# Modulation rows of a hybrid Hyena / FNet / RG-LRU layer on four column groups of the TensorE array

## The chip, the cores and the metric

The kernel runs on one NeuronCore of one Trainium2 chip. The metric is the device time of one launch in microseconds (us), lower is better; each number of a kernel is the median of several runs. For this kernel three runs gave 2820.89 us (2819.37 to 2822.51).

## The reference, cut to what matters

One layer is applied to 1024 latent and 256 context tokens with 1024 channels: a norm with modulation, an input projection that feeds three mixers (a Hyena long convolution, FNet, a bidirectional RG-LRU), their merge, and a SwiGLU block. What the change touches is the modulation alone, six vectors of 1024 values for each of two conditions (latent, context):

```python
mod_ctx = jax.nn.silu(c_ctx[None, :]) @ w_ada[l] + b_ada[l]     # w_ada: 1024 x 6144
mod_lat = jax.nn.silu(c) @ w_ada[l] + b_ada[l]
...
sh1, sc1, g1, sh2, sc2, g2 = jnp.split(mod[:, None, :].astype(dt), 6, axis=-1)
h = rmsnorm(x, n1) * (1 + sc1) + sh1
```

So a product of 2 x 1024 by 1024 x 6144 in fp32, with the result needed channel by channel on the partitions.

## The kernel before, in words

Channels lie on the 128 partitions, tokens along the free dimension. There is one hand-written program for each engine, tied by semaphores; a `wait_ge` holds its whole engine.

The modulation goes through the program in 24 half groups of 256 columns. `csilu` holds silu of both conditions, 8 blocks of 128 channels by 2. `ada_row_unit` (L891) multiplies, for each half group, the 8 blocks `csilu[:, k, :]` (stationary, 128 x 2) with `ada_w[:, k*256:...]` (moving, 128 x 256), all accumulated in rows 0 and 1 of a PSUM bank. ScalarE copies these two rows to `ada_row` in SBUF (L1196, L1259). `ada_turn_unit` (L901) turns them: 128 columns of `ada_row` are the stationary operand, a 2 x 2 identity the moving one, and the result is 128 partitions x 2. VectorE adds the bias into `mod` (`ada_add`, L1504).

Eight half groups are made in the setup, while x is loaded and its squares are summed. The other sixteen are made two at a time in the eight passes of the first stage, `l1_pass` (here "L1 stage", 116 to 575 us). In each pass TensorE's own order is:

- the row unit for two half groups (16 products), then one product `ones` x `ss_k` (L974),
- a wait for `fa_ready`, which VectorE gives at the end of a butterfly (`first_stage`: some forty small VectorE operations at L244 to L256, signalled at L1650), then 24 small DFT products (`fwd_unit`, L953),
- products that make filter taps (`taps_units`, L965), and the input projection of one tile (`projection_tile(2i+1)`, L860 to L862),
- a second wait for `fa_ready`, 24 more DFT products, the turn unit (L906), and the projection of the next tile (`projection_tile(2i+2)`).

ScalarE's order in a pass: copy the rows (L1259), take the root `rs_k` (L1263), copy three pieces of a finished projection from PSUM into `hin` (L1247), which lets GpSimd start; later the copy of a second projection, then the squares of the taps.

GpSimd (POOL) splits each weight tile into a high and a low part (L789, L792) when the projection before it is done, and then computes the short convolution of every other tile (`hy_conv`, L798): it waits for ScalarE's copies into `hin` (L802), and runs two scalings (L805) and ten pairs of a scaling (L811) and an addition (L813).

VectorE's order in a pass: sums and squares of taps (L1643, L1646), butterfly (L244 to L256) and `fa_ready`, a difference (L1651), a reciprocal (L1653), scaled DFT results into `kstage` (L1616), butterfly again and `fa_ready`, taps (L1629), two memsets (L1637, L1638), `kstage` again, the bias addition of the modulation (L1504), the convolution of the other tile (L1588, L1593).

Of the kernel before, what the change touches and what calls it, by code (L numbers as in the profile page):

```python
# [11 lines left out]
ACT = mybir.ActivationFunctionType  # L31
AX_X = mybir.AxisListType.X

P = 128
D = 1024
KD = D // P
# [13 lines left out]
FILT_EMB, FILT_HID = 17, 64  # L50
# [3 lines left out]
HALF_GROUPS = 24  # L54
ADA_FIRST = 8
SQUARES_AT = ((0,), (1, 2), (3, 4), (5,), (6,), (7,), (), ())
FIRST_MIX = 3
MIX_BANKS = 5


V_N1, V_N2, V_FG, V_BADA = 0, KD, 2 * KD, 3 * KD
V_HY = V_BADA + 48
V_LAM = V_HY + 64
V_ALL = V_LAM + 2 * KD

R_CONV, R_CONVB, R_BR, R_BI, R_ST = 512, 516, 517, 519, 521
R_ALL = 523


# [9 lines left out]


TWO_PI = [6.28125, 0.0019350051879882812, 3.0199e-07]
# [6 lines left out]

def real_dft_even(o, z, temp, out):


    e, d = temp(0, 4), temp(4, 8)
    o.add(e, z(0, 4), z(4, 8))
    o.sub(d, z(0, 4), z(4, 8))
    o.sub(out("re4"), temp(0), temp(2))
    o.sub(out("im4"), temp(3), temp(1))
    o.add(temp(8, 10), temp(0, 2), temp(2, 4))
    o.sub(temp(10), temp(5), temp(7))  # L100
    o.add(temp(11), temp(5), temp(7))
    o.add(out("re0"), temp(8), temp(9))
    o.sub(out("re8"), temp(8), temp(9))
    o.mul_add(out("re2"), temp(10), COS[2], temp(4))
    o.mul_add(out("re6"), temp(10), -COS[2], temp(4))
    o.mul_add(out("im6"), temp(11), -COS[2], temp(6))
    o.mul_sub(out("im2"), temp(11), -COS[2], temp(6))


# [26 lines left out]


def real_dft_context(o, z, out):
# [4 lines left out]
    o.mul(out("cim1"), z(1), -1.0)  # L143


# [44 lines left out]


def inverse_context(o, b, temp, y):
# [5 lines left out]


class Chain:  # L200

# [8 lines left out]
    def loose(self, ins):  # L212


        ins.then_inc(self.sem, 1)
        self.n += 1
        if self.n > 1:
            self.eng.wait_ge(self.sem, self.n - 1)
# [15 lines left out]


class Butterfly:

# [17 lines left out]


class MixUnits:

# [15 lines left out]


def places(buf, width, first=0):  # L280
# [8 lines left out]


def spectrum_places(buf):


    def at(name):
        if name.startswith("c"):
            return buf[:, 9 + int(name[3:]), :] if name[1:3] == "re" else buf[:, 19, :]
        f = int(name[2:])
        return buf[:, f if name[:2] == "re" else 11 + f, :]
    return at


# [12 lines left out]

HAS_IMAG = [1 <= q <= 7 or q == 10 for q in range(FH)]
IMAG_AT = {q: (19 if q == 10 else 11 + q) for q in range(FH) if HAS_IMAG[q]}
PAIRS = [(1, 2), (3, 4), (5, 6), (7, 10)]
SINGLES = (0, 8, 9, 11)  # L320


def build_program(nc, dr):

    ctx = ExitStack()
    with ctx:
# [3 lines left out]
        def sb(stack, name, shape, dt=F32):  # L330
            return stack.enter_context(nc.sbuf_tensor(name, shape, dt))


# [5 lines left out]
        vec = sb(ctx, "vec", [P, V_ALL])  # L339
# [10 lines left out]
        cvec = sb(ctx, "cvec", [P, KD, 2])  # L350
        csilu = sb(ctx, "csilu", [P, KD, 2])
        ps = [ctx.enter_context(nc.psum_tensor(f"ps{b}", [P, 512], F32)) for b in range(8)]


# [3 lines left out]
        h2f = filt_ada[0:FILT_HID, :]  # L358
        ada_row = filt_ada[FILT_HID:FILT_HID + 2, 0:512]
        ada_w = [sb(fwd_stack, f"ada_w{s}", [P, KD * 256]) for s in range(2)]  # L360
# [58 lines left out]


        st = ExitStack()
# [13 lines left out]


        low_stack = ExitStack()
# [7 lines left out]
        sq_o, sq_sum = zraw  # L445

# [19 lines left out]
        sq_end_sum = [w_raw[0][:, 0:512], w_raw[0][:, 512:1024], w_raw[1][:, 0:256]]  # L468


# [67 lines left out]

        FILT_UNIT = (0, 1, 2, 4, 5, 7)
# [18 lines left out]
        def raw_z(n):  # L560


            if n == 2:
                return v_b, v_in, 16 * (CH + 1), 0
            if n < 2:
                return zraw[n], zraw_in[n], 16, 0
            slot = (n - 3) % 2
            return zraw[slot], zraw_in[slot], 16 * ((n - 3) // 2 + 2), n - 2 if n < 5 else n - 1

        block = ctx.enter_context(nc.Block())  # L570
        stream = dr["weights"]


        @block.sync
        def _(sp):
# [71 lines left out]


            sp.wait_ge(mod_ready, ADA_FIRST + 8)
# [29 lines left out]


            sp.wait_ge(hy_conved, 1 + TILES_L1)
# [4 lines left out]
            l2_pair(KD // 2 - 1, True)  # L686


# [43 lines left out]


            def load_side(n, src):
# [38 lines left out]


        @block.gpsimd
        def _(pool):
            nc.gpsimd.memset(ones[:], 1.0).then_inc(consts_set, 1)
            nc.gpsimd.memset(eps[:], EPS).then_inc(consts_set, 1)
# [60 lines left out]
            for q in range(FFN_TILES):  # L839


                if q < 2:
                    pool.wait_ge(proj_done[2], OUT_TILE0 + 1 + 31 + q)
                split(MIX_TILES + q, q, wf_hi[q], wf_lo[q])
            with pool.Fori(1, FFN_STEPS) as s:
# [3 lines left out]
                for q in range(FFN_TILES):  # L849
                    pool.wait_ge(*frees[q])  # L850
                    split(FFN_TILES * s + (MIX_TILES + q), q, wf_hi[q], wf_lo[q])


        @block.tensor
        def _(pe):
# [8 lines left out]
            def projection(use, ws, xs, cols, made=None, pieces=(0, 1, 2)):  # L864


                for b in pieces:
                    a, e, _ = PIECES[b]

                    pe.wait_ge(proj_free[b], use)  # L870
                    for k, (w, x) in enumerate(zip(ws, xs)):
                        if made:
                            pe.wait_ge(made, len(xs) * b + k + 1)
                        ins = split_product(ps[b][:, 0:e - a], [w[0][:, cols[k]], w[1][:, cols[k]]],
                                            [x[0][:, a:e], x[1][:, a:e]], k == 0, k == len(ws) - 1)
                    ins.then_inc(proj_done[b], 1)
# [14 lines left out]
            def ada_row_unit(units, it, j, slots, loads):  # L891

                out, done = mix_unit(units, it, j)
                for n, slot in enumerate(slots):
                    pe.wait_ge(ada_in[slot], loads)
                    for k in range(KD):
                        ins = mm(out[0:2, n * 256:(n + 1) * 256], csilu[:, k, :],
                                 ada_w[slot][:, k * 256:(k + 1) * 256], start=k == 0, stop=k == KD - 1)
                ins.then_inc(done, 1)

            def ada_turn_unit(units, it, j, rows, at, width):  # L901

                out, done = mix_unit(units, it, j)
                pe.wait_ge(ada_row_ready, rows)
                for q in range(width // P):
                    ins = mm(out[:, 2 * q:2 * q + 2], ada_row[0:2, at + q * P:at + (q + 1) * P],  # L906
                             ident[FILT_HID:FILT_HID + 2, FILT_HID:FILT_HID + 2],
                             start=True, stop=True)
                ins.then_inc(done, 1)


# [4 lines left out]
            for j, (a, e, _) in enumerate(PIECES):  # L916
                out, done = mix_unit(u_setup, 0, FILT_UNIT[j])
                mm(out[0:FILT_HID, 0:e - a], f_w1[:, :], feats[:, a:e], start=True, stop=True).then_inc(done, 1)
            pe.wait_ge(csilu_set, 1)
            first_rows(0)  # L920
# [10 lines left out]
            for g in range(ADA_FIRST):  # L931
# [3 lines left out]
                if g == ADA_FIRST - 3:  # L935

                    pe.wait_ge(x_sq_summed, KD - 1)
                    for b, (a, e, _) in enumerate(PIECES):
                        mm(ps[b][:, 0:e - a], ones[:], x_sq_sum[:, a:e],
                           start=True, stop=True).then_inc(proj_done[b], 1)  # L940


# [51 lines left out]


            def fnet_channels(c):
# [49 lines left out]


            with pe.Fori(0, CH) as c:
# [39 lines left out]


            z2_pairs = [(z2_hi[:, k, :], z2_lo[:, k, :]) for k in range(4)]  # L1090
# [29 lines left out]
            for p, (a, e, _) in enumerate(PIECES):  # L1120
# [4 lines left out]
                mm(mix(b)[:, 0:e - a], ones[:], sq_sum[:, a:e], start=True, stop=True).then_inc(mix_done[b], 1)  # L1125


# [39 lines left out]


        @block.scalar
        def _(act):  # L1170
# [15 lines left out]


            act.wait_ge(cvec_in, 16)
            fn(csilu[:], cvec[:], ACT.Silu).then_inc(csilu_set, 1)

            def take_row(g):
                src, free = take_mix(u_setup, 0, ROW_UNIT[g])
                if g > 1:

                    act.wait_ge(mod_ready, g - 1)
                own(fn(ada_row[0:2, g % 2 * 256:g % 2 * 256 + 256], src[0:2, 0:256], ACT.Copy))  # L1196
                act.sem_inc(free, 1)
                act.sem_inc(ada_row_ready, 1)
# [40 lines left out]


            act.wait_ge(hin_zero, 1)
# [13 lines left out]
            def l1_pass(i, units, it, last):  # L1255

                src, free = take_mix(units, it, 0)
                act.wait_ge(mod_ready, i + ADA_FIRST)
                own(fn(ada_row[0:2, :], src[0:2, :], ACT.Copy))  # L1259
                act.sem_inc(free, 1)  # L1260
# [17 lines left out]
            l1_pass(7, u1_last, 0, True)  # L1278


# [59 lines left out]


            with act.Fori(0, CH) as c:
# [35 lines left out]


            use0 = OUT_TILE0 + 1  # L1380
# [27 lines left out]
            for p in range(2):  # L1408
                round_normed(p, norm2_u, 3 * KD, u2_ready, h2_hi)


# [32 lines left out]


            act.wait_ge(split_done, N_TILES)
# [11 lines left out]
            for p, (a, e, _) in enumerate(PIECES):  # L1458
                act.wait_ge(ms3_ready, p + 1)
                fn(ps[p][:, 0:e - a], ps[p][:, 0:e - a], ACT.Sqrt, bias=eps[:, 0:1],  # L1460
                   scale=1.0 / D).then_inc(root3_ready, 1)


        @block.vector
        def _(dve):
# [12 lines left out]
            def proj_taken(use):  # L1478

                for b in range(3):  # L1480
                    dve.wait_ge(proj_free[b], use + 1)


# [26 lines left out]
            def softplus():  # L1510

# [168 lines left out]


            for a, e in ((0, PAD_LAT), (PAD_LAT + LAT, PAD_CTX), (PAD_CTX + CTX, PAD_T)):
# [49 lines left out]


            with dve.Fori(0, CH) as c:
# [33 lines left out]
                own.restart()  # L1770


# [77 lines left out]


            def gated_unit(s, n):
# [63 lines left out]

def dft_constants():


# [21 lines left out]


def filter_constants():
# [12 lines left out]


def columns(v):  # L1960

    return np.ascontiguousarray(v.reshape(-1, P).T)


def tiles(w):

    n = w.shape[1] // P
    return w.reshape(KD, P, n, P).transpose(2, 1, 0, 3).reshape(n, P, D)


# [74 lines left out]
```

## Time and profile before

| | |
|---|---|
| median of three runs | 2820.89 us (2819.37 to 2822.51) |
| span of the profiled execution | 2818.3 us (its total is given as this span; the median of the runs is 2.6 us above it) |
| TensorE busy in matmuls | 2576.4 us, 91% |
| VectorE busy | 1579.7 us, 56% |
| GpSimd busy | 884.1 us, 31% |
| ScalarE busy | 559.6 us, 20% |
| L1 stage, 116 to 575 us | TensorE busy 404.29, VectorE 393.75, GpSimd 256.90, ScalarE 49.18 of 459 us |

The share of TensorE is an average over stages. In the L1 stage TensorE and VectorE are both busy for some 86 to 88% of the time, so what counts there is which wait ends last. One product in fp32 shows in the trace as two weight loads (PEld) and two MATMUL records (PE), so the 16 products of a row unit in the L1 stage are 32 records.

### The profile page before, as it was taken

What the parts mean: (1) busy time and instruction counts of PE and PEld (TensorE: products, weight loads), DVE (VectorE), ACT (ScalarE), POOL (GpSimd) and SP (SyncE); (2) the same over time, 40 slices, a digit from 0 to 9 for tenths busy, and PEclk for the clock granted to TensorE, in tenths of its full rate; (3) what the DMA queues carried; (4) which work ended last, traced back from release to release, by engine and by line L of the source; (5) the groups of instructions that cost most, each with busy time, mean ns of one, the idle gap of its engine ahead of it and who ended that gap; (6) DMA issues with size and microseconds to landing.
All of it is one profiled execution on the core that took longest, in us unless ns stands there. A gap on an engine that the chain in (4) does not pass through costs nothing. (4 is left out here: it accounts for less than half of the span.)

```text
span 2818.3 us, 34644 instructions
## 1 busy us (share of the span) xinstructions
PE 2576.4 (91%) x13422; PEld 2141.8 (76%) x13422; DVE 1579.7 (56%) x2636; ACT 559.6 (20%) x825; POOL 884.1 (31%) x483
## 2 busy tenths in 40 slices
PE   6599998999999799999987998979999999999995
PEld 2377776786877688878876887858888888888885
DVE  6888888856568466665666445383322233332227
ACT  3201101045565421122221001130000000000002
POOL 0355455622121122322232332333323133323220
PEclk9799999999999899999998999989999999999998
DMA  6222333122112322222235323211011011101002
GB/s 263 79 96 105 127 122 126 56 96 75 44 68 70 144 92 99 100 91 91 91 119 207 129 86 103 84 45 45 30 45 35 24 45 45 45 30 45 22 22 75
DMA packets 53536, 233.49 MB, mean 83 GB/s; under 512 B 6628, under 2 KB 8548, under 8 KB 47861
## 3 DMA queue, kind: packets, MB, share of 16 engines
q1 hardware_dynamic: 53492, 232.93, 23.0%
q8 instruction: 26, 0.43, 0.1%
q14 instruction: 18, 0.14, 0.0%
HBM read 178.37 MB, written 54.53 MB: 83 GB/s over the span
## 5 line engine op out<-in xcount | busy, mean ns | idle before, releaser
L860 PE MATMUL ps<-h_hi,w_hi 128*128 128x512 f32 (+1 forms) x2256 | 812.1, 360 | 42.5 <-DVE h_lo L1570 18.4
L861 PE MATMUL ps<-h_lo,w_hi 128*128 128x512 f32 (+1 forms) x2256 | 802.4, 356 | 0.0
L862 PE MATMUL ps<-h_hi,w_lo 128*128 128x512 f32 (+1 forms) x2256 | 801.6, 355 | 0.0
L789 POOL TENSOR_TENSOR w_hi<-w_raw,zero_col 128x1024 fp32r<-128x1024 f32 x102 | 229.2, 2247 | 1576.3 <-PE ps L862 1118.0
L860 PEld LDWEIGHTS ps<-h_hi,w_hi 128*128 128x128 f32 x2256 | 428.4, 190 | 116.8 <-issue 28.9
L862 PEld LDWEIGHTS ps<-h_hi,w_lo 128*128 128x128 f32 x2256 | 428.3, 190 | 60.6
L861 PEld LDWEIGHTS ps<-h_lo,w_hi 128*128 128x128 f32 x2256 | 428.9, 190 | 58.4
L1862 DVE TENSOR_TENSOR a<-sil,ps 128x512 f32<-128x512 f32 (+1 forms) x66 | 39.5, 598 | 506.2 <-PE ps L862 505.0
L792 POOL TENSOR_TENSOR w_lo<-w_raw,w_hi 128x1024 fp32r<-128x1024 f32 x102 | 277.1, 2716 | 8.0
L1896 DVE SCALAR_TENSOR_TENSOR x<-ps,mod,x 128x512 f32<-128x512 f32 (+1 forms) x264 | 172.1, 661 | 95.0 <-PE ps L862 94.4
L861 PE MATMUL ps<-h_lo,wf_hi 128*128 128x512 f32 (+1 forms) x528 | 188.7, 357 | 0.0
L860 PE MATMUL ps<-h_hi,wf_hi 128*128 128x512 f32 (+1 forms) x528 | 188.7, 357 | 0.0
L862 PE MATMUL ps<-h_hi,wf_lo 128*128 128x512 f32 (+1 forms) x528 | 188.7, 357 | 0.0
L862 PE MATMUL ps<-act_hi,wf_lo 128*128 128x512 f32 (+1 forms) x528 | 187.0, 354 | 0.0
L861 PE MATMUL ps<-act_lo,wf_hi 128*128 128x512 f32 (+1 forms) x528 | 187.0, 354 | 0.0
L860 PE MATMUL ps<-act_hi,wf_hi 128*128 128x512 f32 (+1 forms) x528 | 186.8, 354 | 0.0
L1429 ACT ACTIVATE sil<-ps 128x512 f32<-128x512 f32 (+1 forms) x66 | 34.7, 527 | 763.1 <-PE ps L862 763.1
L789 POOL TENSOR_TENSOR wf_hi<-w_raw,zero_col 128x1024 fp32r<-128x1024 f32 x44 | 86.2, 1960 | 180.0 <-PE ps L862 180.0
L953 PE MATMUL ps<-f_a,fwd 128*128 128x128 f32 x640 | 90.1, 310 | 53.9 <-DVEq L1650 53.3
L953 PEld LDWEIGHTS ps<-f_a,fwd 128*128 128x128 f32 x640 | 87.9, 225 | 57.3 <-issue 50.3
L860 PEld LDWEIGHTS ps<-h_hi,wf_hi 128*128 128x128 f32 x528 | 100.0, 189 | 15.7
L862 PEld LDWEIGHTS ps<-h_hi,wf_lo 128*128 128x128 f32 x528 | 99.3, 188 | 15.9
(238 smaller groups left out, 3807.7 us busy)
## 6 DMA issues: line engine op xcount, KB each, us to landing
w_raw<-in_weights SPq DMA_DIRECT2D x146, 512.0 KB, 3.7
ada_w<-in_w_ada SPq DMA_DIRECT2D x20, 1024.0 KB, 6.2
scratch_gate_s<-g_st SPq DMA_DIRECT2D x24, 640.0 KB, 3.3
side<-scratch_gate_s SPq DMA_DIRECT2D x24, 640.0 KB, 3.9
scratch_k_s<-kstage SPq DMA_DIRECT2D x8, 1536.0 KB, 5.1
hy_k<-scratch_k_s SPq DMA_DIRECT2D x8, 1536.0 KB, 8.8
scratch_hy_s<-hout SPq DMA_DIRECT2D x16, 640.0 KB, 3.2
x_in<-in_x SPq DMA_DIRECT2D x8, 640.0 KB, 9.1
```

Source lines behind the costliest of these rows:

```text
L789: nc.gpsimd.tensor_tensor(hi[:], w_raw[slot % 2][:], zero_col[:].to_broadcast([P, D]), ALU.add).then_inc(pool_step, 1)
L792: nc.gpsimd.tensor_tensor(lo[:], w_raw[slot % 2][:], hi[:].bitcast(F32), ALU.subtract).then_inc(split_done, 1)
L860: mm(out, w_pair[0], x_pair[0], start=first, stop=False)
L861: mm(out, w_pair[0], x_pair[1], start=False, stop=False)
L862: return mm(out, w_pair[1], x_pair[0], start=False, stop=last)
L953: ins = mm(o, mats[:, q, m, :], part, start=n == 0, stop=n == len(terms) - 1)
L1429: fn(sil[n % 2][:, 0:e - a], ps[b][:, 0:e - a], ACT.Silu).then_inc(f_free[b], 1)
L1862: tt(a32[n % 2][:, 0:e - a], sil[n % 2][:, 0:e - a], ps[ub][:, 0:e - a], ALU.mult).then_inc(f_free[ub], 1)
L1896: stt(x1[:, m, a:e], ps[b][:, 0:e - a], mod[:, 5 * KD + m, seq:seq + 1], x1[:, m, a:e], ALU.mult, ALU.add).then_inc(f_free[b], 1)
```

## The change

Three things are new. The block k of the contraction goes to group `k % 4` of the array's columns: the stationary operand is now `csilu[:, k, :]` with 32 columns (2 values and 30 zeros), and the result lies in PSUM rows 32g to 32g+31, so that blocks 0 and 4 are summed in group 0, 1 and 5 in group 1, and so on. ScalarE copies all 128 rows of the bank, into an `ada_row` that has its own 512 x 4 bytes per partition. The turning product takes all 128 rows of `ada_row` as stationary and a selection matrix of 128 x 2 as moving operand, which adds the four partial rows. The number of products, of copies and their order on each engine stay as they were. A memset of the padding of `csilu` comes at the head of GpSimd's program, TensorE waits once for `vec` before its first row unit, and the scratch reserved for descriptors made on the chip is made smaller to give room.

```diff
+QUAD, QUADS = 32, 4
...
-V_ALL = V_LAM + 2 * KD
+V_SEL = V_LAM + 2 * KD
+V_ALL = V_SEL + 2
...
-        csilu = sb(ctx, "csilu", [P, KD, 2])
+        csilu = sb(ctx, "csilu", [P, KD, QUAD])
...
-        ada_row = filt_ada[FILT_HID:FILT_HID + 2, 0:512]
+        ada_row = sb(fwd_stack, "ada_row", [P, 512])
...
         def _(pool):
+            nc.gpsimd.memset(csilu[:, :, 2:QUAD], 0.0).then_inc(csilu_set, 1)
             nc.gpsimd.memset(ones[:], 1.0).then_inc(consts_set, 1)
...
                     for k in range(KD):
-                        ins = mm(out[0:2, n * 256:(n + 1) * 256], csilu[:, k, :],
-                                 ada_w[slot][:, k * 256:(k + 1) * 256], start=k == 0, stop=k == KD - 1)
+                        g = k % QUADS
+                        ins = mm(out[QUAD * g:QUAD * g + QUAD, n * 256:(n + 1) * 256], csilu[:, k, :],
+                                 ada_w[slot][:, k * 256:(k + 1) * 256], start=k < QUADS, stop=k >= KD - QUADS)
                 ins.then_inc(done, 1)
...
-                    ins = mm(out[:, 2 * q:2 * q + 2], ada_row[0:2, at + q * P:at + (q + 1) * P],
-                             ident[FILT_HID:FILT_HID + 2, FILT_HID:FILT_HID + 2],
-                             start=True, stop=True)
+                    ins = mm(out[:, 2 * q:2 * q + 2], ada_row[:, at + q * P:at + (q + 1) * P],
+                             vec[:, V_SEL:V_SEL + 2], start=True, stop=True)
...
-            pe.wait_ge(csilu_set, 1)
+            pe.wait_ge(csilu_set, 2)
+            pe.wait_ge(vec_in, 16)
             first_rows(0)
...
-            fn(csilu[:], cvec[:], ACT.Silu).then_inc(csilu_set, 1)
+            fn(csilu[:, :, 0:2], cvec[:], ACT.Silu).then_inc(csilu_set, 1)
...
-                own(fn(ada_row[0:2, g % 2 * 256:g % 2 * 256 + 256], src[0:2, 0:256], ACT.Copy))
+                own(fn(ada_row[:, g % 2 * 256:g % 2 * 256 + 256], src[:, 0:256], ACT.Copy))
...
-                own(fn(ada_row[0:2, :], src[0:2, :], ACT.Copy))
+                own(fn(ada_row[:, :], src[:, :], ACT.Copy))
...
+    sel = np.zeros((P, 2), np.float32)
+    for g in range(QUADS):
+        sel[QUAD * g, 0] = sel[QUAD * g + 1, 1] = 1.0
...
-    nc = bacc.Bacc("TRN2", target_bir_lowering=False, num_devices=1)
+    nc = bacc.Bacc("TRN2", target_bir_lowering=False, num_devices=1, dynamic_dma_scratch_size=2048)
```

## Rows read from the trace of the kernel before

**Rows 1.** Instructions that use `csilu`, whole run (duration ns min/median/max, first and last start us).

```profile
L897 PEld LDWEIGHTS ps<-ada_w,csilu x320: 80/85/130, 11.8 to 538.3; 128*2 128x2 f32 x160
L897 PE MATMUL ps<-ada_w,csilu x320: 377/379/635, 11.8 to 538.5; 128*2 128x256 f32 x160
```

**Rows 2.** TensorE in order of time, one pass (start us, us; in brackets idle before).

```profile
357.38 0.28 PE L862 MATMUL ps<-h_hi,w_lo 128*128 128x256 f32 x1
357.59 7.07 PE L897 MATMUL ps<-ada_w,csilu 128*2 128x256 f32 x32
364.59 0.70 PE L974 MATMUL ps<-ss_k,ones 128*128 128x256 f32 x2
371.42 6.38 PE L953 MATMUL ps<-f_a,fwd 128*128 128x128 f32 x40 [6.13 <-DVEq L1650]
...
396.13 4.63 PE L953 MATMUL ps<-f_a,fwd 128*128 128x128 f32 x40
415.68 7.07 PE L897 MATMUL ps<-ada_w,csilu 128*2 128x256 f32 x32
```

**Rows 3.** VectorE at the end of that pass's second part, in order of time.

```profile
396.81 0.17 DVE L1638 MEMSET taps<- 1x128 f32 x1
397.89 0.69 DVE L1616 TENSOR_TENSOR kstage<-ps,rs_k 128x512 f32<-128x512 f32 x1 [0.91 <-PE ps L953]
```

**Rows 4.** ScalarE and GpSimd behind the row unit in the same pass.

```profile
360.25 2.47 POOL L792 TENSOR_TENSOR w_lo<-w_raw,w_hi 128x1024 fp32r<-128x1024 f32 x1
364.78 0.58 ACT L1259 ACTIVATE filt_ada<-ps 2x512 f32<-2x512 f32 x1 [19.65 <-PE ps L897]
365.55 0.47 ACT L1263 ACTIVATE rs_k<-ps,eps 128x256 f32<-128x256 f32 x1 [0.19 <-ACT filt_ada L1259]
365.92 1.35 ACT L1247 ACTIVATE hin<-ps 128x512 f32<-128x512 f32 x3
367.62 0.42 POOL L802 COPY hy_taps<-vec 128x4 f32 x1 [4.89 <-ACT hin L1247]
368.14 2.30 POOL L805 TENSOR_SCALAR hout<-hin,hy_taps 128x1024 f32<-128x1024 f32 x2
```

**Rows 5.** VectorE and GpSimd where both run, same pass: butterfly operations with and without company.

```profile
362.93 0.28 DVE L247 TENSOR_TENSOR f_t<-f_t 128x128 f32<-128x128 f32 x1
368.65 1.12 DVE L244 TENSOR_TENSOR f_a<-f_t 128x128 f32<-128x128 f32 x1
...
380.95 0.73 POOL L813 TENSOR_TENSOR hout<-hout,hy_part 128x256 f32<-128x256 f32 x1
381.02 0.81 DVE L247 TENSOR_TENSOR f_t<-f_t 128x128 f32<-128x128 f32 x1
382.16 0.48 DVE L247 TENSOR_TENSOR f_a<-f_t 128x128 f32<-128x128 f32 x1
383.03 0.81 POOL L813 TENSOR_TENSOR hout<-hout,hy_part 128x256 f32<-128x256 f32 x1
```

**Rows 6.** First DFT batch of passes 0, 2 and 6, of eight, TensorE.

```profile
136.96 7.51 PE L953 MATMUL ps<-f_a,fwd 128*128 128x128 f32 x40 [10.51 <-DVEq L1650]
254.95 6.58 PE L953 MATMUL ps<-f_a,fwd 128*128 128x128 f32 x40 [6.19 <-DVEq L1650]
487.60 6.32 PE L953 MATMUL ps<-f_a,fwd 128*128 128x128 f32 x40 [6.14 <-DVEq L1650]
```

**Rows 7.** Stretches of one pass: busy of PE, PEld, DVE, ACT, POOL; granted clock; DMA.

```profile
371.40:374.80 3.40, 3.38 (x16) 3.39 (x17) 3.22 (x2) 0.00 (x0) 3.13 (x4) 0.50 0.25 106
374.90:377.70 2.80, 2.80 (x26) 2.71 (x25) 1.38 (x2) 0.00 (x0) 2.52 (x4) 1.00 0.00 0
```

**Rows 8.** Setup: the sum of squares' product and what follows it, in order of time.

```profile
39.17 5.90 PE L897 MATMUL ps<-ada_w,csilu 128*2 128x256 f32 x16
...
56.52 2.42 PE L939 MATMUL ps<-x_sq_sum,ones 128*128 128x512 f32 x6 [1.08 <-DVE x_sq_sum L1543]
57.74 1.28 ACT L1223 ACT_TABLE_LOAD   x1 [2.40 <-PE ps L939]
```

More of the change, by code:

```diff
@@ L2000 @@
     lam = np.asarray(rg_lam)[0].reshape(2, KD, P).transpose(2, 1, 0).reshape(P, 16)
+    sel = np.zeros((P, 2), np.float32)
+    for g in range(QUADS):
+        sel[QUAD * g, 0] = sel[QUAD * g + 1, 1] = 1.0
     vec = np.concatenate([columns(np.asarray(norm1_g)[0]), columns(np.asarray(norm2_g)[0]),
-                          columns(np.asarray(final_g)), columns(np.asarray(b_ada)[0]), hy, lam], axis=1)
+                          columns(np.asarray(final_g)), columns(np.asarray(b_ada)[0]), hy, lam, sel], axis=1)
     wr, wi = np.asarray(rg_wr)[0], np.asarray(rg_wi)[0]
```

## The prediction

> **What bounds the kernel now.** I read the tile view of `csilu` first, for what the changed products cost. A row unit's products show as records of 379 ns with weight loads of 85 ns [rows 1]. The modelled ends overlap, so the price is taken from the order of time: 32 records in 7.07 us, 0.22 us from one to the next [rows 2]. Eight such units in the L1 stage and eight of half the size in the setup make some 86 us of TensorE, 3% of the span. If TensorE were the bound everywhere, this would be the place to save.
>
> The order of time in one pass says otherwise. Behind the row unit and one small product, TensorE stands idle for 6.13 us until VectorE's butterfly gives `fa_ready` [rows 2]. The idle time is there in all eight passes (6.19 us in pass 2, 6.14 in pass 6, 10.51 in pass 0 [rows 6]). A shorter row unit makes this wait longer and nothing earlier. From `fa_ready` on TensorE is the one who sets the pace: DFT batch, taps, projection and second DFT batch run without a gap to 400.7, and VectorE, done with its memsets at 396.98, waits 0.91 us for the second batch [rows 2, 3]. So a pass is one chain: VectorE to the first `fa_ready`, TensorE to the second DFT batch, VectorE again. The row unit is not in it.
>
> Who does wait for the row unit is ScalarE, 19.65 us [rows 4]. Behind its copy stand the root and the three copies into `hin`, and behind these GpSimd, which starts its convolution 2.96 us after the row unit's end (367.62 against 364.66) and had been idle for 4.89 us [rows 2, 4].
>
> That start matters, since GpSimd's work slows VectorE. A butterfly operation of 0.28 us takes 1.12 us beside the first scaling L805, 0.84 more; 0.81 us, or 0.53 more, beside an addition L813; and 0.48 us, or 0.20 more, beside a scaling L811 [rows 4, 5]. One pair of L811 and L813 takes 2.08 us (380.95 to 383.03) and costs VectorE 0.73 us [rows 5]. The Trainium skill ("SBUF — State Buffer", its part on the engine and DMA sides) calls the port pair that VectorE and GpSimd share an exclusive lock, where the loser blocks for the whole instruction; the trace agrees in kind, with these 0.20 to 0.84 us.
>
> **The change, part by part.**
>
> *Row unit.* Not in the trace is how products in different column groups overlap. The bounds from rows: nothing gained, 7.07 us; or four at once, a quarter, 1.8 us; or worse than now, with no load hidden, 32 x (0.085 + 0.379) = 14.8 us [rows 1, 2]. I take half. The two records of one block need the same columns and follow each other as now; only the first record of the next block can run beside the second of this one. So 16 blocks x 0.22 = 3.5 us and a tail of 0.2: 3.7 us. The row unit ends 3.4 us earlier.
>
> The Trainium skill ("TensorE: Matmul & The Clock Gate", Part 3) gives 2.38 times for three column tiles with 512 moving columns, one pass each; that rate would give 7.07 / 2.38 = 3.0 us as an estimate, and the result would be a further 0.7 us of shift and some 0.3 us more per pass.
>
> *ScalarE's copies* stay at one instruction with as many columns: 0.58 us for 2 x 512, and the three copies into `hin`, of 128 rows and 1280 columns, take 1.35 us [rows 4]. Zero. *Turn unit*: same number of loads of 128 columns and of products of 2; zero, bounds plus or minus 0.1 us per pass. *Memset, wait for `vec`, smaller scratch, padding columns*: once each, under the loads of the setup; zero, plus or minus 0.2 us.
>
> *GpSimd's start.* In passes 1 to 7 it moves from 367.62 to about 364.2, 3.4 us earlier; it is free from 362.72 on, where its split ends [rows 4]. So it can come at most 4.9 us earlier. In pass 0 the small product L974 waited for VectorE's sums anyway, so nothing moves.
>
> *VectorE before `fa_ready`.* Now it has from 368.14 to 371.4 company of the two L805 (0.84 + 0.20) and the start of one L811 (0.20): 1.24 us. After the change the two scalings are over by 367.1, and until the butterfly's end come two whole pairs and one more L811: 1.04 + 2 x 0.73 + 0.20 = 2.7 us. That is 1.5 us more per pass, and it is on the chain. What GpSimd then no longer does at its end, near 390, falls where VectorE waits for TensorE anyway and gives nothing back. Seven passes: 7 x 1.5 = **10.5 us**. Bounds: 0.7 us per pass if the row unit only falls to 5.5 us, 1.9 us if it falls to a quarter.
>
> *TensorE's clock after the wait.* The first DFT batch takes 6.38 us and the same batch behind a projection 4.63 [rows 2]; the granted clock is 0.50 (1.2 GHz) for the first 3.4 us and 1.00 (2.4 GHz) after [rows 7]. The passes of before came to rest at nearly the lowest price, from 7.51 us in pass 0 to 6.58 and then 6.32 [rows 6], and a pass takes 58.09 us there (357.59 to 415.68 [rows 2]). A pass that is longer by 1.5 us has no reason to rest there. I take 7.0 us, near the middle of 6.32 and 7.51, for a mean of about 6.5 now: 0.5 x 7 = **3.5 us**. Bounds 0 and 7 x 1.0 = 7 us.
>
> *Setup.* The eight half-size row units lie beside the chain of ScalarE's squares and VectorE's sums, and none of them is waited for on it. But they keep TensorE's clock up: one unit ran at the low clock in 5.90 us for the usual half of 7.07, and the product of the squares, for whose first third ScalarE waits 2.40 us, took 2.42 us at the high one [rows 8]. With less work before it that product may meet the low clock; its first piece (512 of 1280 columns) is then 0.97 us later: **1.0 us**, bounds 0 and 1.0.
>
> Sum: 10.5 + 3.5 + 1.0 = 15.0 us on the span of 2818.3, so 2833.3; the median of the runs lies 2.6 us above that span, which gives **2836 us**, 0.53% slower. The case's own range is 0.7 x 7 = 4.9, so 2826, to 7 x 1.9 + 7 + 1 = 21.3, so 2842.
>
> **The rivals.** *A, the column groups do not overlap* and the row unit stays near 7 us. Nothing moves, 2821 us. For it: nothing in this trace shows two products at once. *B, the row unit halves but the chain does not feel it*, because GpSimd's earlier operations find gaps. Then too 2821 to 2822 us. Against it: the stretched operations of rows 5 are in the same butterfly, with the same neighbours.
>
> *C, faster: the row unit becomes longer*, from changes of group and loads of 32 columns that are no longer hidden. GpSimd then starts later, and VectorE sheds the 1.24 us before `fa_ready`: 7 x 1.24 = 8.7 us, so 2812 us. It holds from about 10.3 us per unit (3.2 us later) to 13.2 us, where the idle 6.13 us are used up; at 14.8 us TensorE itself is 1.6 us late and the gain is gone. A row that speaks against it: the last record of 128 columns starts at 357.38 and takes 0.28, the first of 2 columns follows at 357.59 [rows 2], so changing the width costs nothing seen. The Trainium skill ("TensorEngine Tiling (Array Packing)", Key Properties) says that a change of tiling mode drains the array; no run here shows the price with column groups, and by that rule this rival would gain some weight.
>
> *D, faster: TensorE's saved time counts in full*, 8 x 3.4 + 8 x 1.7 = 41 us, so 2780 us. Against it stand the eight idle stretches of 6 us and more behind the row unit.
>
> **How the numbers follow.** The forecast gets 0.57, A 0.20, B 0.12, C 0.08, D 0.03. About 0.2%, 5.6 us, is what a measurement here can tell from no change. Slower by more than that: the forecast without its low end, 0.54. Within: A, B and that end, 0.35. Faster: C and D, 0.11. The range takes in A and B with their scatter and the forecast up to its bound, and leaves out D, most of C and a little above: 2817 to 2842 us.
>
> **What would show it.** The row unit should read about 3.7 us for 32 records, with ScalarE's wait for it falling from 19.65 to about 16 to 18 us; GpSimd's `hy_taps` copy should start some 3.4 us earlier against the row unit's begin; VectorE should reach `fa_ready` 15.3 us after the row unit's begin (now 13.8); and TensorE's idle time should read about 11 us. The forecast is wrong if the row unit stays at 7 us, or if it falls and `fa_ready` does not move.

## The result and the profile after

The changed kernel takes **2841.14 us** in the median of four runs (2837.57 to 2843.57), beside 2821.33 us (2819.37 to 2822.51) for the kernel before on the same chip: a ratio of 1.0069, 95% interval 1.0054 to 1.0083, so slower by some 20 us. The span of its profiled execution is 2838.2 us, 19.9 us more than the 2818.3 of before. The busy times from the page, and the tile view of `csilu`, which answers to [rows 1]:

```profile
PE 2526.3 (89%) x13422; PEld 2126.4 (75%) x13422; DVE 1579.0 (56%) x2636; ACT 559.3 (20%) x825; POOL 872.7 (31%) x484
```

```profile
L836 PEld LDWEIGHTS ps<-ada_w,csilu x320: 106/110/178, 11.2 to 552.4; 128*32 128x32 f32 x160
L836 PE MATMUL ps<-ada_w,csilu x320: 378/379/637, 11.2 to 552.6; 128*32 128x256 f32 x160
```

TensorE is busy for 50 us less than before (2526.3 against 2576.4), with as many records, and the kernel is longer. A record is as long as before, 379 ns, and its load is 25 ns longer; what changed is how many run at once. That stands only in the order of time. TensorE in pass 5 of the L1 stage, with the second batch, the turn unit and the next row unit, answers to [rows 2]:

```profile
428.02 0.28 PE L801 MATMUL ps<-h_hi,w_lo 128*128 128x256 f32 x1
428.23 1.93 PE L836 MATMUL ps<-ada_w,csilu 128*32 128x256 f32 x32
...
445.01 7.06 PE L890 MATMUL ps<-f_a,fwd 128*128 128x128 f32 x40 [14.22 <-DVEq L1571]
...
470.43 4.62 PE L890 MATMUL ps<-f_a,fwd 128*128 128x128 f32 x40
474.89 0.95 PE L845 MATMUL ps<-vec,ada_row 128*128 128x2 f32 x8
...
489.67 1.94 PE L836 MATMUL ps<-ada_w,csilu 128*32 128x256 f32 x32
```

The row unit takes 1.93 us where it took 7.07: 60 ns a record. Eight records in each group at 0.22 us are 1.77 us, so by this count the four groups ran side by side all the time, apart from a tail. The idle stretch behind it grew from 6.13 to 14.22 us: by the 5.14 us that the unit no longer takes, and by 2.95 us more. From the row unit's begin to the first DFT batch it is 16.78 us, where it was 13.83; the batch itself takes 7.06 (6.38), and the whole pass 61.44 us (58.09).

ScalarE and GpSimd behind the same row unit answer to [rows 4] (a count after x says how many instructions a row stands for):

```profile
430.31 0.60 ACT L1189 ACTIVATE ada_row<-ps 128x512 f32<-128x512 f32 x1 [14.24 <-PE ps L836]
...
430.45 2.67 POOL L733 TENSOR_TENSOR w_lo<-w_raw,w_hi 128x1024 fp32r<-128x1024 f32 x1
433.16 0.19 POOL L743 COPY hy_taps<-vec 128x4 f32 x1
433.46 2.48 POOL L746 TENSOR_SCALAR hout<-hin,hy_taps 128x1024 f32<-128x1024 f32 x2
436.04 1.15 POOL L752 TENSOR_SCALAR hy_part<-hin,hy_taps 128x256 f32<-128x256 f32 x1
...
443.62 0.80 POOL L754 TENSOR_TENSOR hout<-hout,hy_part 128x256 f32<-128x256 f32 x1
```

GpSimd now goes from its split straight into the convolution: the copy of `hy_taps` starts 4.93 us after the row unit's begin (433.16 less 428.23), where it was 10.03 us. It is 5.1 us earlier and waits for nothing. Below is VectorE's butterfly, first as it was before in the pass of [rows 2] (its first operation, and the difference behind `fa_ready`), then now:

```profile
357.13 0.69 DVE L244 TENSOR_TENSOR f_t<-tsum 128x512 f32<-128x512 f32 x1
...
371.38 1.49 DVE L1651 TENSOR_TENSOR tsum<-taps 128x1280 f32<-128x1280 f32 x1
```

```profile
427.93 0.69 DVE L210 TENSOR_TENSOR f_t<-tsum 128x512 f32<-128x512 f32 x1 [0.15 <-DVE ss_k L1567]
...
433.95 0.28 DVE L210 TENSOR_TENSOR f_t<-f_t 128x128 f32<-128x128 f32 x1
434.15 1.12 DVE L210 TENSOR_TENSOR f_a<-f_t 128x128 f32<-128x128 f32 x1
...
439.55 0.81 DVE L213 TENSOR_TENSOR f_a<-f_t 128x128 f32<-128x128 f32 x1
...
443.76 0.81 DVE L213 TENSOR_TENSOR f_a<-tsum 128x128 f32<-128x128 f32 x1
...
444.97 1.49 DVE L1572 TENSOR_TENSOR tsum<-taps 128x1280 f32<-128x1280 f32 x1
```

It took 14.25 us and now takes 17.04. The stretched operations are those of [rows 5], with the same lengths: 1.12 us beside the scaling that starts at 433.46, and 0.81 us beside each addition L754 (439.55 beside the one at 439.47, 443.76 beside the one at 443.62). Between 433.46 and 444.97 lie both scalings L746 and four whole pairs: 1.04 + 4 x 0.73 = 4.0 us, against 1.24 before, so 2.8 us. The work that GpSimd now does early is missing later: VectorE's second butterfly of the pass takes 10.3 us (453.12 to 463.42) where it took 13.2 (378.86 to 392.05). That gives nothing back, since VectorE then waits for TensorE's second batch, 3.84 us where it was 0.91 in [rows 3]:

```profile
472.19 0.69 DVE L1537 TENSOR_TENSOR kstage<-ps,rs_k 128x512 f32<-128x512 f32 x1 [3.84 <-PE ps L890]
```

**The balance.** The first DFT batch of pass 0 starts at 139.18 us (136.96), that of pass 7 at 567.06 (545.24): 2.2 us late becomes 21.8. Between them lie seven pass lengths: the stretch from row unit to batch is some 2.9 us longer in each (20.0 us), the seven first batches of passes 0 to 6 are together 1.7 us longer, and the stretch from the second batch over the turn unit to the next row unit is 0.3 us shorter in each (2.1 us). That is 2.2 + 20.0 + 1.7 - 2.1 = 21.8 us. What comes after, the rest of pass 7 and all later stages, gives 1.9 us back, which I can't explain.

### The profile page after: what moved, and what is told of

Its sections match the earlier page's. It is cut to its first block and busy times, and to the rows that moved or that the text cites. A ratio compares the mean times of both kernels' runs of the same rounds, so it can differ in the third digit from the quotient of the medians.

```text
span 2838.2 us, 34646 instructions
## 1 busy us (share of the span) xinstructions
PE 2526.3 (89%) x13422; PEld 2126.4 (75%) x13422; DVE 1579.0 (56%) x2636; ACT 559.3 (20%) x825; POOL 872.7 (31%) x484
## 5 line engine op out<-in xcount | busy, mean ns | idle before, releaser
L800 PEld LDWEIGHTS ps<-h_lo,wf_hi 128*128 128x128 f32 x528 | 99.3, 188 | 16.0
```

Source lines behind the costliest of these rows:

```text
L800: mm(out, w_pair[0], x_pair[1], start=False, stop=False)
```

## The experiments

The theory: **contention**. The row unit held GpSimd's convolution back; shortened, it lets the convolution start inside VectorE's butterfly, which is on the path ("Theory 1" in the expectations). The rivals: **idle** ("Theory 2": TensorE stands still for longer, its clock falls, and everything behind is slower) and **groups** ("Theory 3": the form itself, with its scratch, padding and layout, costs time elsewhere). The first seven kernels tell these apart; the others look for what is left and for a version that gains.

**e1_gate** holds the convolution behind the butterfly.

```diff
                     if s == 0:
+                        pool.wait_ge(fa_ready, 2 * i + 1)
                         hy_conv(2 * i, 2 * i + 1)
```

> The changed kernel, but GpSimd's convolution also waits for the first fa_ready of the pass. Theory 1 (the convolution that starts early stalls VectorE's butterfly): the butterfly loses all company of the convolution, 4.0 us per pass against the changed kernel (its 2.8 us of loss and the 1.24 us that the kernel before had too); fa_ready comes about 12.8 us after the row unit's begin instead of 16.8. How much of it reaches the time depends on the first DFT batch: at the 7.05 us of the changed kernel a pass takes 57.4 us and the time is about 2813 us; if the batch grows again, up to 8 us, because the pass ends where the clock does not rise yet (theory 1 with the clock holding the pass), a pass stays at 58.0 us and the time is 2817 to 2820 us. Theory 2 (the longer idle time of TensorE and its clock are the loss): idle time falls only from 14.2 to 10.2 us, the batch stays at 7 us, the time stays above 2830 us. Theory 3 (layout, scratch size or the column groups themselves): stays at 2841 us.

Measured: 2815.49 us (ten runs), ratio 0.9982 (0.9972 to 0.9992) to the kernel before, so some 25 us under the changed kernel. TensorE and GpSimd:

```profile
412.86 1.93 PE L837 MATMUL ps<-ada_w,csilu 128*32 128x256 f32 x32
...
425.63 7.66 PE L891 MATMUL ps<-f_a,fwd 128*128 128x128 f32 x40 [10.21 <-DVEq L1572]
```

```profile
425.76 1.37 POOL L743 COPY hy_taps<-vec 128x4 f32 x1 [8.00 <-DVEq L1572]
```

The batch starts 12.77 us after the row unit's begin, not 16.78: all contention with the convolution is gone, the 1.24 us of before too (what the weight splits cost the butterfly stays; e9 takes that out). The time lies between the two that I had named for this theory. One wait takes the whole loss away while the groups stay: contention is shown as the main cause.

**e2_repeat4** runs the L1 stage's row products four times over, in their groups, so that the unit has its old length (the cut shows the factor written out, here and in e8; the setup keeps 1).

```diff
-                    for k in range(KD):
+                    for k in list(range(KD)) * 4:
```

> The changed kernel with the row products of the L1 stage done four times over, so that the row unit takes about 7.6 us on four column groups (7.07 before, 1.93 changed). Theory 1: GpSimd's convolution starts where it started before, the butterfly takes 14.2 us again, a pass takes 58.1 us, and the time is 2820 to 2823 us (setup 1 to 2 us later, turn unit 0.3 us per pass shorter). Theory 3 (layout, scratch size, column groups themselves): 2838 us or more. Theory 2 (TensorE's idle time): also back to about 2822 us, since the idle time is short again; so this run tells theory 3 from the other two only.

Measured: 2820.80 us, ratio 0.9998 (0.9988 to 1.0007).

```profile
418.06 7.11 PE L836 MATMUL ps<-ada_w,csilu 128*32 128x256 f32 x128
...
432.10 6.46 PE L890 MATMUL ps<-f_a,fwd 128*128 128x128 f32 x40 [6.30 <-DVEq L1571]
```

Four times the work costs nothing; it gives the 20 us back, and the pass is that of before (58.07 us). The rival "groups" falls.

**e3_fill56** leaves contention as it is and fills TensorE's idle time with products of no use, in another bank.

```diff
                 mm(out[:, 0:2 * P], ones[:], ss_k[:, :, :], start=True, stop=True).then_inc(done, 1)
+                out, done = mix_unit(units, it, 2)
+                for _ in range(56):
+                    mm(out[:, 0:P], ones[:], ones[:], start=True, stop=True)
```

> The changed kernel with 56 products of ones by ones (128 columns, about 0.23 us each, 12.9 us) put between the small product behind the row unit and the wait for fa_ready, so that TensorE idles about 1.3 us instead of 14.2. Theory 1: the butterfly keeps its 17.0 us and fa_ready comes 16.8 us after the row unit's begin as now; only the first DFT batch falls from 7.05 to 4.6 to 5 us; a pass takes 59.0 us, minus 2.3 us times 8, plus 3 us in pass 0 where the fill is too long: 2824 to 2828 us. Theory 2 (idle time and clock are the whole loss): back to 2821 us or below, with fa_ready earlier too. A sign of theory 1 is that the butterfly does not change at all.

Measured: 2827.88 us, ratio 1.0020 (1.0011 to 1.0030).

```profile
422.34 1.93 PE L836 MATMUL ps<-ada_w,csilu 128*32 128x256 f32 x32
...
439.05 4.73 PE L890 MATMUL ps<-f_a,fwd 128*128 128x128 f32 x40 [1.65 <-DVEq L1574]
```

The stretch from row unit to batch stays 16.71 us. With 1.65 us idle the batch takes 4.73 us instead of 7.06, so the clock is worth 2.3 us per pass here, and the butterfly does not change. The two causes are separate. But a batch of 6.4 us was paid before as well, so of the change's 20 us the idle time explains only the batches' 1.7 to 2.6.

**e4_gate_before** puts the same wait into the kernel before, without groups.

```diff
+                        pool.wait_ge(fa_ready, 2 * i + 1)
                         hy_conv(2 * i, 2 * i + 1)
```

> The kernel before, with GpSimd's convolution also waiting for the first fa_ready of the pass. Theory 1: the butterfly loses 1.24 us per pass, fa_ready comes 12.6 us after the row unit's begin instead of 13.8. If this reaches the time in full, 8.7 us: 2812 us. If the clock holds the pass (the first DFT batch begins earlier but the clock rises at the same moment), the batch grows from 6.4 to 7.5 to 8.8 us and the time is 2819 to 2822 us. Theory 2: no change of the butterfly and none of the time.

Measured: 2814.87 us, ratio 0.9979 (0.9970 to 0.9989), again between my two figures.

```profile
412.91 7.07 PE L898 MATMUL ps<-ada_w,csilu 128*2 128x256 f32 x32
...
425.56 7.47 PE L954 MATMUL ps<-f_a,fwd 128*128 128x128 f32 x40 [4.96 <-DVEq L1651]
```

The same as with groups within 1 us. In both, the stretch to the batch is 1.1 to 1.2 us shorter than before, and in the later passes the batch is longer by about as much (7.47 and 7.66 against 6.38), so the pass stays at 58.0 us. What e1 gains against e2 is made in the first passes: the first batch of pass 0 starts 2.6 us earlier (137.01 against 139.57), that of pass 2 5.5 us (251.95 against 257.45), and the distance grows only to 6.5 us by pass 6 (483.62 against 490.16).

**e5_gate_fill_before** and **e6_gate_fill_after** keep the waits of e4 and e1 and add filling products ahead of the `ss_k` product, 16 and 40, so that VectorE alone sets the batch's start and TensorE hardly rests.

```diff
+                out, done = mix_unit(units, it, 2)
+                for _ in range(16):    (40 in e6)
+                    mm(out[:, 0:P], ones[:], ones[:], start=True, stop=True)
                 out, done = mix_unit(units, it, 1)
                 pe.wait_ge(ss_ready, i + 1)
```

> The kernel before, with GpSimd's convolution held until the first fa_ready and 16 products of ones by ones (3.7 us) between the row unit and the small product L974, so that TensorE idles about 1.2 us instead of 4.9. If the clock held the passes of e4 at 58.0 us, this frees them: first DFT batch 4.7 us instead of 7.5, a pass 55.3 us, eight times 2.7 us less than e4: 2793 to 2796 us. If the clock did not hold them and something else fixed 58.0 us, the batch falls and another wait grows by as much: 2812 us or more.

> The changed kernel with the same two edits, 40 products (9.2 us) since its row unit is shorter. Theory 1: butterfly without company, first DFT batch 4.7 us, a pass about 55.0 us: 2790 to 2795 us, so the changed kernel is no better than the kernel before once both are freed, within 3 us (turn unit 0.35 us per pass shorter, setup 1 to 2 us longer). If the column groups have a worth of their own that was hidden until now, it is 10 us or more below e5.

Measured: 2798.04 us (0.9919, 0.9903 to 0.9936) and 2797.24 us (0.9915, 0.9898 to 0.9931), both some 2 us above the upper end of what I expected. Without groups, then with them:

```profile
346.11 7.07 PE L898 MATMUL ps<-ada_w,csilu 128*2 128x256 f32 x32
...
358.63 4.73 PE L954 MATMUL ps<-f_a,fwd 128*128 128x128 f32 x40 [1.25 <-DVEq L1654]
...
401.23 7.07 PE L898 MATMUL ps<-ada_w,csilu 128*2 128x256 f32 x32
```

```profile
358.72 4.73 PE L891 MATMUL ps<-f_a,fwd 128*128 128x128 f32 x40 [1.19 <-DVEq L1575]
```

The batch is down to 4.73 us and the pass to 55.1 us (401.23 less 346.11). And the groups bring nothing even here, where the earlier end of the row unit no longer sets GpSimd's start: e6 is less than 1 us under e5, of 23 us that both gain.

**e7_setup3** repeats the setup's row products three times, to see whether less work in the setup slows what follows there.

```diff
-                    for k in range(KD):
+                    for k in list(range(KD)) * times:    (3 in the setup, 1 in the passes)
```

> The changed kernel with the row products of the setup alone done three times over (about 2.8 us per unit, 3.6 before, 0.9 to 1.9 changed). The product of the squares should run at the high clock again, 2.42 us instead of 4.63, and VectorE's norm should begin about 1 us earlier; the L1 stage as in the changed kernel, 61.4 us per pass. Time 2837 to 2841 us. If the setup's clock matters for nothing, the norm begins at the same moment.

Measured: 2839.20 us, 1.0071 (1.0055 to 1.0088): no different from the changed kernel. The squares' product and VectorE's reciprocal behind it, after and then in e7:

```profile
55.87 4.63 PE L877 MATMUL ps<-x_sq_sum,ones 128*128 128x512 f32 x6 [1.93 <-DVE x_sq_sum L1464]
...
60.05 8.53 DVE L1470 RECIPROCAL rstd<-rstd 128x512 f32<-128x512 f32 x3 [4.16 <-ACT rstd L1154]
```

```profile
55.85 2.42 PE L877 MATMUL ps<-x_sq_sum,ones 128*128 128x512 f32 x6 [0.20 <-DVE x_sq_sum L1464]
...
59.08 8.53 DVE L1470 RECIPROCAL rstd<-rstd 128x512 f32<-128x512 f32 x3 [3.21 <-ACT rstd L1154]
```

The setup term is real in the trace: the product took 4.63 us for 2.42, and the reciprocal starts 0.97 us later. At 1 us it is too small to be seen in the times. That it is the clock is not shown: the product has the length that half the clock would give, but the granted clock (third number from the end) reads 1.00 beside it in both, after and then e7:

```profile
57.00:58.00 1.00, 1.00 (x3) 0.48 (x2) 0.00 (x0) 0.00 (x0) 0.00 (x0) 1.00 0.02 8
```

```profile
57.00:58.00 1.00, 1.00 (x4) 0.39 (x3) 0.00 (x0) 0.94 (x1) 0.00 (x0) 1.00 0.08 33
```

**e8_double_before** doubles the row products of the kernel before in the L1 stage, which is 56 us more work for TensorE.

```diff
-                    for k in range(KD):
+                    for k in list(range(KD)) * 2:
```

> The kernel before with the row products of the L1 stage done twice, a row unit of 14.1 us, 56 us more work for TensorE. Theory 1: GpSimd's convolution comes 7 us later, after the butterfly, which loses its 1.24 us; TensorE gets to the first DFT batch without idle time, 14.8 us after the row unit's begin instead of 13.8, and does it in 4.7 us instead of 6.4; a pass takes 57.3 to 57.6 us and the time is 2813 to 2818 us, faster than before. If TensorE's work were the bound: 2877 us. If only the company of the convolution counted and not the clock: 2828 us.

Measured: 2807.37 us, ratio 0.9954 (0.9937 to 0.9970); some 6 us better than the best I had expected. TensorE, then GpSimd and VectorE:

```profile
407.53 13.97 PE L897 MATMUL ps<-ada_w,csilu 128*2 128x256 f32 x64
...
421.97 4.63 PE L953 MATMUL ps<-f_a,fwd 128*128 128x128 f32 x40
```

```profile
424.46 0.19 POOL L802 COPY hy_taps<-vec 128x4 f32 x1 [12.04 <-ACT hin L1247]
```

```profile
420.24 1.49 DVE L1651 TENSOR_TENSOR tsum<-taps 128x1280 f32<-128x1280 f32 x1
```

This is the change turned round. The longer unit holds GpSimd back behind the butterfly, VectorE is ready 12.7 us after the row unit's begin (420.24 less 407.53), and TensorE, now 1.7 us late itself, goes into the batch warm: 4.63 us, at a granted clock of 1.00 (422.0 to 426.5).

**e9_split_late, e10_conv_first, e11_conv_first_fill32** (changed kernel) and **e12_conv_first_before** (kernel before) also take GpSimd's first split out of the butterfly. e9 is e6 with the wait ahead of the split and 24 filling products instead of 40; e10 to e12 do the convolution first and the split behind it, with 24, 32 and 8 filling products. The edit of GpSimd's program in e10 to e12 (the filling products stand where they do in e5):

```diff
                     pool.wait_ge(proj_done[2], 2 * i + (2 + s))
-                    split(2 * i + (2 + s), s, w_hi[s], w_lo[s])
                     if s == 0:
+                        pool.wait_ge(fa_ready, 2 * i + 1)
                         hy_conv(2 * i, 2 * i + 1)
+                    split(2 * i + (2 + s), s, w_hi[s], w_lo[s])
```

> The kernel of e6, with GpSimd's first weight split of a pass held until fa_ready as well, before the convolution, and 24 products of ones by ones instead of 40. Theory 1 says that a split stalls VectorE as the convolution does (1.7 and 2.15 us in the butterfly): the butterfly takes about 9.3 us instead of 13.0. GpSimd then ends its convolution some 30 us after fa_ready, 1 to 2 us after TensorE wants the banks for the next projection, so a new wait of TensorE gives part back: a pass of 52.5 to 53.5 us and a time of 2779 to 2785 us. If GpSimd's end costs more than the butterfly gains: 2797 us or more.

> As e9, with the convolution first and the split behind it. The banks come free 26.5 us after fa_ready, in time; the split is ready 30 us after it, about 1 us after TensorE wants it. A pass of 52 to 53 us and a time of 2775 to 2782 us. If the later split collides with VectorE's kstage and convolution instead, nothing is gained on e9.

> The kernel of e10 with 32 products of ones by ones instead of 24, so that TensorE idles some 0.5 us instead of 2.3 to 3.0 before the first DFT batch. If that remaining idle time is what lets the clock fall in e10 (its batches read 4.73 to 7.63 us), the batch reads 4.7 us in every pass, a pass takes about 52.5 us and the time is 2778 to 2783 us. If the clock falls for another reason, 2793 us stays.

> The kernel before with the edits of e11, and 8 products of ones by ones, since its row unit is 5.1 us longer. If the column groups are worth nothing even with VectorE and the clock freed, this is within 3 us of e11. If they are worth something at last, because the wait for fa_ready is now short, e11 is 5 us or more below this.

Measured: 2800.63 us (0.9928, 0.9911 to 0.9945), 2793.24 (0.9895, 0.9878 to 0.9911), 2790.35 (0.9897, 0.9881 to 0.9914) and 2789.76 (0.9896, 0.9879 to 0.9912). The first batch in e9 and in a late pass of e10, then two lines of TensorE in e11:

```profile
410.13 6.36 PE L892 MATMUL ps<-f_a,fwd 128*128 128x128 f32 x40 [2.73 <-DVEq L1576]
```

```profile
407.79 7.63 PE L891 MATMUL ps<-f_a,fwd 128*128 128x128 f32 x40 [3.04 <-DVEq L1575]
```

```profile
287.05 1.93 PE L837 MATMUL ps<-ada_w,csilu 128*32 128x256 f32 x32
...
298.04 4.73 PE L891 MATMUL ps<-f_a,fwd 128*128 128x128 f32 x40 [1.28 <-DVEq L1575]
```

The butterfly shrank as expected, to 9.2 us in e9, but the times of e9, e10 and e11 lie 16, 11 and 7 us above the upper ends of what I expected. Part is the clock: with 2.73 and 3.04 us idle the batch is slow again in e9 and e10, with 1.28 us in e11 it is not. But e11, with the first batch of every pass but pass 0 at 4.73 us, is only 3 us under e10, and its ratio to the kernel before is no better (0.9897 against 0.9895), so most of what the clock gave there was taken elsewhere. Part lies behind the second batch, where VectorE scales `hout` for its own convolution. That operation in e6, then in e9, then in e11:

```profile
388.55 1.14 DVE L1513 TENSOR_SCALAR hout<-hin,vec 128x1024 f32<-128x1024 f32 x2 [0.89 <-DVE mod L1431]
```

```profile
442.37 2.16 DVE L1514 TENSOR_SCALAR hout<-hin,vec 128x1024 f32<-128x1024 f32 x2 [1.67 <-DMA scratch_hy_s<-hout]
```

```profile
327.82 3.63 DVE L1513 TENSOR_SCALAR hout<-hin,vec 128x1024 f32<-128x1024 f32 x2 [0.86 <-DVE mod L1431]
```

The work that left the butterfly comes down here: in e11 GpSimd's splits, now behind the convolution, stretch the scaling from 1.14 to 3.63 us in this pass, and in e9 it is stretched by 1.0 us and waits 0.8 us longer, for the transfer of the last `hout`.

e10, e11 and e12 are the fastest versions found, some 30 us under the kernel before and not told apart by their ratios; e11 against e12 says again that the groups make no difference.

## Why the prediction came out as it did

- **The bound of a pass**: right. The pass is a chain of VectorE, TensorE, VectorE without the row unit in it: e2 puts four times the products into it at no cost, e8 speeds the kernel up with more of them.
- **Row unit, 7.07 to 3.7 us**: mis-sized, it is 1.93 us, near the bound of 1.8. The step that failed is "only the first record of the next block can run beside the second of this one": all four groups run side by side. The estimate of 3.0 us from the Trainium skill ("TensorE: Matmul & The Clock Gate", Part 3) was nearer and still too long: 7.07 / 1.93 is 3.66 times with four groups.
- **GpSimd's start, 3.4 us earlier**: it is 5.1 us, all of the bound of 4.9 and a little more.
- **VectorE before `fa_ready`, 1.5 us more per pass and 10.5 in all**: the mechanism is right and shown by e1 and e2; the size was 2.8 us of butterfly per pass, and 20.0 us over seven passes with what lies around it. It is above my bound of 1.9 us as well. The term that was too small is the count "two whole pairs and one more L811": there are four pairs. For one part GpSimd starts 5.1 us earlier and not 3.4. The rest is that even the bound for the earliest start, 1.9 us, took a butterfly of the old length, and one that is slowed down lasts into further operations of GpSimd: by that the fixed window undercounts 0.9 us of the 2.8.
- **Clock after the wait, 3.5 us**: the eight batches together went from 52.96 to 55.56 us, 2.6 us. The batch did come to rest at about 7.0 us (7.06 in pass 5). The granted clock is at the low level for longer than the 3.4 us of [rows 7]: it reads 0.50 up to 449.60, 4.6 us after the batch's start:

```profile
445.00:448.40 3.40, 3.39 (x16) 3.40 (x17) 3.21 (x2) 0.00 (x0) 3.13 (x4) 0.50 0.00 0
...
449.00:449.60 0.60, 0.60 (x4) 0.60 (x4) 0.27 (x1) 0.00 (x0) 0.60 (x1) 0.50 0.00 0
```

- **Setup, 1.0 us**: the size is as said, by e7; that the clock is the cause stays open, as said there. The unit of 5.90 us that I took as one at the low clock has a mean granted clock of 0.60 (39.20 to 45.00). The first batch of pass 0 is 2.2 us late, and the other 1.2 us is no more than profiles of the same code differ by: the row unit of pass 0 begins at 116.81 us in the profile of before and at 118.26 to 118.89 in e4, e5, e8 and e12, which have the same code up to there (119.11 in the changed kernel).
- **Turn unit, zero**: its stretch gave 0.3 us per pass back, above my bound of 0.1. It takes 0.95 us instead of 1.05, and VectorE's bias addition no longer waits for it.
- **Rivals**: A (no overlap) falls by 1.93 us. B (not felt) falls by the butterfly. C (row unit longer) is false of this change, but its mechanism is real: e8 lengthened the unit by 6.9 us and gained 13 us, more than the 8.7 I gave it, since the batch then takes 4.63 us too. It did so at 13.97 us per unit, beyond the 13.2 us up to which I had let this rival hold. The drain that the Trainium skill tells of ("TensorEngine Tiling (Array Packing)", Key Properties) can't be seen: the first record in a column group starts 0.21 us behind the last of 128 columns (428.23 less 428.02), as the narrow one did before. D (all of TensorE's time counts) falls with 50 us less busy time and 20 us more span.
- **The signs**: ScalarE's wait for the row unit fell to 14.24 us (said 16 to 18), GpSimd's copy came 5.1 us earlier (3.4), `fa_ready` 16.8 us after the row unit's begin (15.3), TensorE's idle time is 14.2 us (11): all the way that was forecast, and all further.
- **The number**: the butterfly term was 9.5 us too small (10.5 for 20.0) and the start 1.2 us. Against this stand 0.9 us too much for the clock, 2.1 us in the stretch of the turn unit and 2.8 us behind the first batch of pass 7 (the 1.9 us of the balance, counted from that batch's end and not its start), neither of which I had in the sum: 9.5 + 1.2 - 0.9 - 2.1 - 2.8 = 4.9. So 2841 lies 5 us above the forecast, at the upper edge of the range: right in sign and mechanism, low in size. That it lies inside is in part luck, since without the last two it would be 2846.

Left open: why a pass rests at 58.0 us in before, e1, e2 and e4, though butterfly and idle time differ among them, and at 61.4 with the changed one; the 1.9 us given back; what makes the setup's product slow; how the misses of e9 to e11 divide.

## What to carry to other kernels

Before an off-path unit is made shorter, ask which engine's start it holds back, and what that engine will then run beside: here 5.1 us less on TensorE let GpSimd into VectorE's critical stretch and cost 20 us, and one wait on GpSimd gave 25 us back. Where the engine that waits also has a clock to lose, take away the contention and the idle time together: on the kernel before, the wait alone gave 6 us, the wait with filling products 23 us (filling products alone were run only on the changed kernel, where they gave 13). Count contention against the stretched work, not against its old length.

## What was not expected of the hardware

- Four column groups of 32 columns run side by side in fp32, 3.66 times as fast as one after the other: 32 records of 379 ns in 1.93 us, with the blocks of one unit laid over the groups in turn. A load of 32 columns takes 110 ns where one of 2 took 85.
- The price of the first batch follows no simple rule of the idle time before it: 14.22 us idle gave 7.06, 10.21 gave 7.66, 4.96 gave 7.47, 6.13 gave 6.38 us. After 1.19 to 1.65 us (e3, e5, e6, e11) the batch took 4.73 us, after 2.73 us in e9 6.36 us. Two passes of e10, one after the other, with the same idle time:

```profile
300.02 6.36 PE L891 MATMUL ps<-f_a,fwd 128*128 128x128 f32 x40 [2.32 <-DVEq L1575]
...
354.20 4.73 PE L891 MATMUL ps<-f_a,fwd 128*128 128x128 f32 x40 [2.33 <-DVEq L1575]
```

- What GpSimd costs VectorE goes by the kind of operation: 0.84 us beside the first scaling of a convolution, 0.53 beside an addition, 0.20 beside a scaling, in both kernels. Such a scaling itself takes 0.92 us and such an addition 0.73 where nothing slows them, so VectorE is held for less than GpSimd's whole instruction, which "agrees in kind" in the prediction passes over.
- TensorE can be given 56 us of useless work and the kernel is 13 us faster (e8).
